# Scaling x by its inverse rms before a transpose, in place of products with a diagonal, at three seams of a two-layer decoder trunk

## The reference, cut to what matters

```
h = rmsnorm(x, pre_g) * (1 + scale) + shift      # rmsnorm: x * rsqrt(mean(x*x) + eps) * g
y = mixer(h)      or      conv_glu(h)
x = x + gate * rmsnorm(y, post_g)
```

## Time and profile before

| | |
|---|---|
| median of 3 runs | 1005.71 us (1005.63 to 1005.88) |
| the profiled execution | 1003.84 us |
| its span (first to last instruction) | 1002.2 us |
| mean granted TensorE clock | 0.989 of full |
| PE busy | 948.2 us (95%) |
| PEld busy | 882.0 us (88%) |
| DVE busy | 723.7 us (72%) |
| ACT busy | 525.0 us (52%) |
| POOL busy | 43.6 us (4%) |
| all of L1596 (diagonal products), PE | 19.9 us, 128 records |

### The profile page before, as it was taken

How to read it: one execution, slowest core, us unless ns; L and a number is a source line. 1 busy time by engine, 2 the same in 40 slices (tenths; PEclk the granted TensorE clock), 3 DMA queues, 4 the chain that set the end, 5 groups by cost and what they waited for, 6 DMA issues and landing times.

```text
span 1002.2 us, 17710 instructions
## 1 busy us (share of the span) xinstructions
PE 948.2 (95%) x6896; PEld 882.0 (88%) x6896; DVE 723.7 (72%) x962; ACT 525.0 (52%) x698; POOL 43.6 (4%) x85
## 2 busy tenths in 40 slices
PE   2599999999998999999989999999999999999997
PEld 2499989999987999999969999899999799999996
DVE  5879856667676988788776866667667689666675
ACT  3345756445447555454564475753445656454544
POOL 0000000000000100000000000000100000000000
PEclk9799999999999999999999999999999999999999
DMA  9986655655572786767635863556746557555541
GB/s 356 348 249 215 198 188 163 215 190 192 178 264 82 273 275 247 236 247 250 233 124 174 274 225 120 175 174 219 238 133 229 186 191 271 186 182 179 181 152 43
DMA packets 134137, 206.85 MB, mean 206 GB/s; under 512 B 6208, under 2 KB 104256, under 8 KB 133952
## 3 DMA queue, kind: packets, MB, share of 16 engines
q1 hardware_dynamic: 122416, 162.59, 49.6%
q0 software_dynamic: 11520, 41.95, 11.4%
q10 hardware_dynamic: 144, 1.51, 0.4%
HBM read 204.98 MB, written 1.05 MB: 206 GB/s over the span
## 4 chain that ended last, share of the span: by engine, by line
PE 89%; DVE 4%; ACT 3%; issue 1%; DMA 1%; SPq 0%; DVEq 0%; ACTq 0%
PE banks L1580 79%; PE banks L1596 2%; DMA raw<-in_ada_rows 1%; DVE w_lo L1020 1%; PE banks L1845 1%; PE banks L1848 1%; PE banks L1604 1%; PE banks L1689 1%; PE banks L1671 1%; ACT h L577 1%; ACT w_hi L529 1%; PE banks L1708 1%; DVE x L1110 0%; PE banks L1717 0%; PE banks L1734 0%
## 5 line engine op out<-in xcount | busy, mean ns | idle before, releaser
L1580 PE MATMUL banks<-h_lo,w_hi 128*128 128x256 f32 x1504 | 430.9, 287 | 2.9 <-DVE h_lo L1081 2.9
L1580 PE MATMUL banks<-h_hi,w_lo 128*128 128x256 f32 x1504 | 426.1, 283 | 0.0
L1580 PE MATMUL banks<-h_hi,w_hi 128*128 128x256 f32 x1504 | 425.9, 283 | 0.0
L1580 PEld LDWEIGHTS banks<-h_lo,w_hi 128*128 128x128 f32 x1504 | 288.7, 192 | 6.6 <-DVE h_lo L1081 3.7
L1580 PEld LDWEIGHTS banks<-h_hi,w_lo 128*128 128x128 f32 x1504 | 288.8, 192 | 2.3 <-issue 1.4
L1580 PEld LDWEIGHTS banks<-h_hi,w_hi 128*128 128x128 f32 x1504 | 288.8, 192 | 0.0
L1020 DVE TENSOR_TENSOR w_lo<-raw,w_hi 128x2048 fp32r<-128x2048 f32 x82 | 187.0, 2289 | 70.8 <-ACT w_hi L529 70.8
L529 ACT ACTIVATE w_hi<-raw 128x2048 fp32r<-128x2048 f32 x82 | 155.7, 1909 | 107.9 <-PE banks L1580 105.1
L1519 DVE TENSOR_TENSOR w_lo<-raw,w_hi 128x2048 fp32r<-128x2048 f32 x56 | 128.0, 2286 | 24.7 <-ACT w_hi L905 24.7
L905 ACT ACTIVATE w_hi<-raw 128x2048 fp32r<-128x2048 f32 x56 | 107.0, 1910 | 45.6 <-PE banks L1580 45.6
L1496 DVE SCALAR_TENSOR_TENSOR EF<-banks,par,EF 128x254 f32<-128x254 f32 (+1 forms) x176 | 76.8, 478 | 51.0 <-ACT EF L886 45.6
(11 more groups left out here) (262 smaller groups left out, 1226.0 us busy)
## 6 DMA issues: line engine op xcount, KB each, us to landing
raw<-in_w_in SPq DMA_DIRECT2D x52, 1024.0 KB, 5.6
raw<-in_ffn_w_up SPq DMA_DIRECT2D x44, 1024.0 KB, 5.1
adw<-in_ada_rows POOLq DMA_DIRECT2D x80, 512.0 KB, 4.7
raw<-in_ffn_w_down SPq DMA_DIRECT2D x22, 1024.0 KB, 4.9
raw<-in_w_out SPq DMA_DIRECT2D x8, 1024.0 KB, 7.0
raw<-in_ret_wo SPq DMA_DIRECT2D x4, 1024.0 KB, 5.0
raw<-in_lru_wo SPq DMA_DIRECT2D x4, 1024.0 KB, 6.7
raw<-in_mla_wo SPq DMA_DIRECT2D x4, 1024.0 KB, 7.2
```

What stands on the lines that cost most here:

```text
L1580: ins = MM(ps, lhs, rhs, start=first and n == 0, stop=last and n == 2)
```

## The change

Two tiles' worth of `EF` serve as buffers for scaled x, one of 1024 columns for each chunk (`scaled(c)`). At the three seams VectorE no longer builds the diagonal: after the reciprocal it multiplies columns 512 to 1023 of x by it, and ScalarE multiplies columns 0 to 511. TensorE transposes the eight pieces of the result; the first four wait for ScalarE's half, the other four for VectorE's. The first two calls, before layer 0, keep the diagonal. ScalarE's new step, `scale_rows`, stands between the two last `post_square` for chunk 0; for chunk 1 it stands between the two `h_high` of chunk 0 (ph = 0) or after the last `square` (ph = 1). It waits for VectorE's reciprocal.

```diff
+        n_xa, n_xd = sig("n_xa", 4), sig("n_xd", 4)
...
+        def scaled(c):
+            return EF[:, 4 * c:4 * c + 4, :].rearrange("p a b -> p (a b)")
...
+            def scale_rows(l, n, c):
+                act.wait_ge(n_rs.s, n_rs.at(l, n + 1))
+                A_(scaled(c)[:, 0:512], x[:, c, 0:512], ACT.Copy, scale=st[:, 4 + c:5 + c]).then_inc(n_xa.s, 1)
...
                 square(l2, n, 0, 1)
                 post_square(l, ph, 1, 0)
+                scale_rows(l2, n, 0)
                 post_square(l, ph, 1, 1)
                 act.wait_ge(mod_ready.s, mod_ready.at(l, ph + 2))
                 if ph == 0:
...
                     h_high(l2, n, 0, 0)
+                    scale_rows(l2, n + 1, 1)
                     h_high(l2, n, 0, 1)
                 else:
...
                     square(l2, n + 1, 1, 1)
+                    scale_rows(l2, n + 1, 1)
                 for half in range(2):
...
                 dve.wait_ge(n_rs.s, n_rs.at(l, n + 1))
-                V.tensor_scalar(diag[:, c, :], ident, st[:, 4 + c:5 + c], None, ALU.mult).then_inc(n_dg.s, 1)
+                if l == 0 and n < 2:
+                    V.tensor_scalar(diag[:, c, :], ident, st[:, 4 + c:5 + c], None, ALU.mult).then_inc(n_dg.s, 1)
+                else:
+                    V.tensor_scalar(scaled(c)[:, 512:1024], x[:, c, 512:1024], st[:, 4 + c:5 + c], None, ALU.mult).then_inc(n_xd.s, 1)
...
             def to_features(l, n, c):
-                pe.wait_ge(n_dg.s, n_dg.at(l, n + 1))
+                first = l == 0 and n < 2
+                if first:
+                    pe.wait_ge(n_dg.s, n + 1)
                 for half in range(2):
+                    if not first:
+                        sg = (n_xa, n_xd)[half]
+                        pe.wait_ge(sg.s, sg.at(l, n - 1))
                     for k in range(4):
                         kk = 4 * half + k
                         bank, i = (ACT_BANK if k < 2 else DVE_BANK)[c][half], k % 2
-                        ins = MM(PS[:, bank, P * i:P * i + P], x[:, c, P * kk:P * kk + P], diag[:, c, :], start=True, stop=True)
+                        if first:
+                            ins = MM(PS[:, bank, P * i:P * i + P], x[:, c, P * kk:P * kk + P], diag[:, c, :], start=True, stop=True)
+                        else:
+                            ins = nc.tensor.transpose(PS[:, bank, P * i:P * i + P], scaled(c)[:, P * kk:P * kk + P], ident)
                     ins.then_inc(n_tp.s, 1)
```

## The result

Slower, outside the range. The changed kernel took 1011.50 us in the median of 12 executions (1004.95 to 1012.08), the kernel before 1006.04 (1005.63 to 1006.86, 12 executions): ratio 1.0036, interval 1.0024 to 1.0048. (The ratios here weigh all executions, and so lie near the ratio of the means; that of these two medians would be 1.0054.) The forecast was 1006.9, no change. The executions don't scatter evenly.

| executions of 24 | time, us | mean granted clock |
|---|---|---|
| 4 | 1004.5 to 1005.1 | 0.987 to 0.988 |
| 8 | 1006.8 to 1008.1 | 0.985 to 0.987 |
| 12 | 1011.2 to 1012.1 | 0.982 |

The account below looks back on a forecast made before the run. Time was taken to move only when TensorE's stream of products starts later or earlier. 0.44 + 0.27 + 0.44 = +1.15 us on the profiled 1003.84 gave 1004.99, plus 1.87 for the runs' median: 1006.9 us, range 1005.3 to 1009.0.

Parts of the forecast that it names:

- (a): Six altered calls: 16 TensorE records become 8 transposes; a half takes 0.71 us instead of 1.15, 0.44 less on the path.
- (b): Six altered calls: a ScalarE scaling copy of 0.71 us replaces the 0.29 us diagonal on the path; VectorE's half takes 0.49.
- Outer seams: First and third seam: the up-projection starts 0.44 us later in each, by 0.22 to 0.62 depending on ScalarE's scale time.
- chunk 0: First chunk in the outer seams: costs nothing, first half of transposes done at 312.91 us against 312.97 for the products.
- the cover: First seam: VectorE's 1.11 us wait before its next reciprocal, said to hide the 0.8 us it starts later.
- +0.50: Outer seams, chunk 1: VectorE's modulation starts 0.50 us later, after the delayed second h_hi and its h_lo.
- Second seam: After layer 0's MLP: transposes start about 1.15 us later, the call is 0.90 shorter, the next product starts 0.27 us later.
- The sum with the clock of the kernel before: All three seams with the granted clock unchanged: +1.15 us in total, bounds 0.5 to 1.7.
- the clock stays: Main forecast, all seams: granted clock unchanged, no added fall to 1.2 GHz; 1006.9 us, chance 0.52.
- the first clock rival: Second seam: a 2.3 us TensorE wait halves the clock once more, +1.65 us, 1008.5 us in all; chance 0.27.
- the outer rival: Outer seams: transposes and thinner fillers fail to hold the clock, 1.7 us each, +3.4, 1010.3 us in all; chance 0.12.
- TensorE's time is what counts: All seams: 48 fewer records save 5.3 us, copies cost 2.5; 2.8 us faster, 1002.9 us; chance 0.06.

Follow-up runs that it names:

- the filled pair: Kernel before and changed kernel, each with TensorE fillers added in every wait of the seams: 1004.62 us (ratio 0.9989) and 1006.95 us (ratio 1.0007).
- run 20: Not a follow-up run: a verb and a count, TensorE had run 20 products of one column, 2.39 us, in the kernel before.

## Why the prediction was wrong, by its own steps

- **(a), (b): right.** Eight records a call in 1.06 to 1.09 us in the outer seams; the scale 0.717 us against 0.71; VectorE's half 0.487 against 0.49. Taking the operand's price from the earlier trace rows paid.
- **Outer seams: +0.44 forecast, +0.30 and +0.29 measured.** The part mis-sized is chunk 0, booked as free. From reciprocal to reciprocal it takes 5.19 us (313.67 to 318.86), and took 5.33: the second half of the transposes is there sooner, so that ScalarE's four modulations take 1.50 us and not the 1.64 of the earlier trace rows. It gains 0.14. The 0.8 us that VectorE loses behind the new wait came as forecast, and nearly all the cover is used: it stood 1.11 us ahead of the second reciprocal, now it comes to it straight from its modulations. (In chunk 1 the forecast goes from +0.50 to +0.44 and does not say why; +0.44 was right.)
- **Second seam: +0.27 forecast, +0.29 without a second fall** (15.33 against 15.04), +1.02 with one. The agreement is partly luck: both these profiles have a fall at the first call, and without any (the filled pair) it is +0.68, as the kernel before has 14.64 and the changed one 15.32. ScalarE's weight block starts 1.72 us after the reciprocal and not 0.35 (+1.37, forecast +1.4).
- **The sum with the clock of the kernel before: right in size.** 0.87 us measured, 1.15 forecast (1.28 in the filled pair). The second profile of the changed kernel took 1007.16 us, and eight of 24 executions lie from 1006.8 to 1008.1.
- **What failed: "the clock stays" as the likeliest case.** The waits themselves were forecast: 2.3 us (2.11 measured), 1.7 (1.79), 1.8 to 2.0 (1.89). In the one profile of the longest group the clock fell in all three places; that it did so in all of the group's executions, half of the 24, is inferred from their equal times and mean clock (0.982). I priced the second seam's fall (+1.65, chance 0.27) and the outer ones' (+3.4, 0.12) as cases that exclude each other. They can come together: 1.15 + 1.65 + 3.4 = 6.2 gives 1011.9 us, and the longest group lies at 1011.2 to 1012.1. No case of the forecast had that sum, and the range ended at 1009.0. The price per fall was about right: 1.46 and 1.48 us measured in the MLP stretches, 1.70 in the second seam and behind it (0.73 + 0.97), against 1.7 forecast.
- **What the first clock rival took from its rows was too simple.** It weighed the chance of a fall by the length of the wait alone. The trace of the kernel before has a fall at 604.5 us, shortly before which TensorE had not waited but run 20 products of one column, 2.39 us:

```profile
600.99 2.39 PE L1734 MATMUL banks<-cst,tmp 128*128 128x1 f32 x20
604.50:607.90 3.40, 3.40 (x18) 3.40 (x17) 3.40 (x5) 1.39 (x3) 0.00 (x0) 0.50 0.26 25
```

- **Half of the reason given for the outer rival was wrong.** The thinner work and longer waits were right, the part on transposes was not. Sixteen transposes cost no more than sixteen products in three pairs of runs (1008.47 against 1008.50, 1009.20 against 1010.55, 1009.42 against 1012.30 us), and the clock fell with products alone. The Trainium skill, "TensorE: Matmul & The Clock Gate", Part 4, says that a transpose doesn't count as busy in the same way; these three pairs don't bear that out.
- **"TensorE's time is what counts": wrong, as the forecast had judged.** With 48 records fewer the kernel did not get faster. The shorter calls do shorten the path (0.73 us in an outer seam, from 12.26 to 11.53), which pays for most of the ScalarE copy; but they also leave TensorE waiting where the old products had filled time.

## What to carry to other kernels

Where an engine is only busy to keep its clock, its instructions are not to be counted as cost: a shorter one on TensorE must be paid back with fillers, and each wait that an edit lengthens past what the trace has shown to be harmless is to be priced with a fall behind it, and the case in which all of them fall is to be in the forecast. Read the granted clock of several executions, not one, before two profiles are subtracted. And a copy moved to another engine brings that engine's queue with it: here the engine that computed the factor was also the best one to apply it.

## What the runs showed of the hardware that was not expected

- Whether a wait of about 2 us brings TensorE to 1.2 GHz differs from one execution of the same program to the next: the changed kernel's two profiles have the same waits (1.79 and 1.89 us in the first seam, 2.11 and 2.13 in the second), and behind these waits and those of the third seam three falls in one and none in the other.
- The clock also falls where TensorE is hardly ever idle: at about 121 us, in or just behind a stretch of small products (64-row and one-column ones), in 13 of the 18 profiles and not in that of the kernel before. Behind the same code of layer 1, at 601 to 609 us, 9 of the 18 have one, that of the kernel before among them.
- Scaling 128x512 f32 from SBUF by a factor per row takes ScalarE 0.717 us (0.625 for `h_hi`, which has no factor and writes float32r) and VectorE 0.487.
